# Hybrid attention and MoE step on one Trainium2 core: the sample's rows first in the last projection block

## The reference, cut to what matters

```
z = hn @ w_in
fq, fk, fv, ff, dq, dk, dv = jnp.split(z, SPLITS, axis=-1)
...
dk = _rope(_rms(dk.reshape(n_b, n_t, DIFF_HEADS, 2, HEAD_DIM), dk_g), pos)
dk = dk.reshape(n_b, n_t, DIFF_HEADS, 2 * HEAD_DIM)
dv = dv.reshape(n_b, n_t, DIFF_HEADS, 2 * HEAD_DIM)
```

## Time and profile before

| What | us |
|---|---|
| median of three runs | 1353.77 (1352.5 to 1355.65) |
| the profiled execution, its own time | 1354.91 |
| its span, first to last instruction | 1353.0 |
| TensorE busy | 1288.7 |
| VectorE busy | 377.3 |
| ScalarE busy | 209.9 |
| GpSimd busy | 145.0 |

### The profile page before, as it was taken

How to read it: one execution, slowest core, us unless ns; L and a number is a source line. 1 busy time by engine, 2 the same in 40 slices (tenths; PEclk the granted TensorE clock), 3 DMA queues, 4 the chain that set the end, 5 groups by cost and what they waited for, 6 DMA issues and landing times.

```text
span 1353.0 us, 16150 instructions
## 1 busy us (share of the span) xinstructions
PE 1288.7 (95%) x6083; PEld 573.3 (42%) x6084; DVE 377.3 (28%) x958; ACT 209.9 (16%) x524; POOL 145.0 (11%) x340
## 2 busy tenths in 40 slices
PE   6799999999998999999999999999999999999997
PEld 3344444565454433434344343443434344343432
DVE  3213223557252322213222121311212132121212
ACT  5111322346150101101001010100101010010100
POOL 0021300000004101011010110101011010101000
PEclk9899965579998999999999999999999999999998
DMA  8901440036525999999999999999999999999994
GB/s 286 323 29 74 174 168 1 0 128 226 209 70 210 431 427 427 428 429 429 428 430 428 428 429 429 428 428 430 428 428 430 428 429 428 430 428 427 429 426 183
DMA packets 54537, 447.06 MB, mean 330 GB/s; under 512 B 10817, under 2 KB 11090, under 8 KB 29922
## 3 DMA queue, kind: packets, MB, share of 16 engines
q1 hardware_dynamic: 54498, 446.54, 79.4%
HBM read 441.66 MB, written 4.86 MB: 330 GB/s over the span
## 4 chain that ended last, share of the span: by engine, by line
PE 65%; DMA 25%; SPq 4%; DVE 2%; POOL 1%; issue 1%; ACT 1%; DVEq 0%; POOLq 0%; ACTq 0%
DMA arena<-in_w_gate_up 23%; PE psum L1588 17%; PE psum L1556 16%; PE psum L1537 7%; PE psum L1303 5%; PE psum L1451 3%; PE psum L1407 3%; PE psum L1603 2%; PE psum L1359 2%; SPq L390 2%; PE psum L1387 1%; PE psum L1339 1%; PE psum L1571 1%; PE psum L1567 1%; PE psum L1355 1%; SPq L406 1%
## 5 line engine op out<-in xcount | busy, mean ns | idle before, releaser
L1556 PE MATMUL psum<-arena 128*64 128x512 f32 x2048 | 450.5, 599 | 18.9 <-DMA arena<-in_w_gate_up 18.4
L1556 PEld LDWEIGHTS psum<-arena 128*64 128x64 f32 x2048 | 152.9, 138 | 314.7 <-issue 314.7
L1588 PE MATMUL psum<-arena 128*64 128x512 f32 x1024 | 224.8, 597 | 0.8
L1210 DVE TENSOR_SCALAR arena<-psum 128x256 f32<-128x256 f32 x64 | 26.7, 418 | 432.4 <-PE psum L1556 430.6
L1588 PEld LDWEIGHTS psum<-arena 128*64 128x64 f32 x1024 | 78.8, 138 | 136.0 <-issue 134.6
L1303 PE MATMUL psum<-arena 128*128 128x512 f32 x288 | 127.6, 599 | 0.0
L838 ACT ACTIVATE arena<-arena 128x256 f32<-128x256 f32 x64 | 26.7, 418 | 630.5 <-DVE arena L1210 630.5
L1537 PEld LDWEIGHTS psum<-arena 128*128 128x128 f32 x768 | 88.5, 194 | 16.1 <-issue 16.1
L1537 PE MATMUL psum<-arena 128*128 128x128 f32 x768 | 91.6, 279 | 3.8 <-POOL arena L604 3.8
L1603 PE MATMUL psum<-arena 128*128 128x512 f32 x192 | 93.2, 623 | 0.0
L597 POOL COPY arena<-arena 128x6 f32 (+1 forms) x16 | 3.0, 188 | 775.6 <-PE psum L1588 703.5
(11 more groups left out here) (215 smaller groups left out, 905.2 us busy)
## 6 DMA issues: line engine op xcount, KB each, us to landing
arena<-in_w_gate_up SPq DMA_DIRECT2D x128, 2048.0 KB, 25.0
arena<-in_w_down SPq DMA_DIRECT2D x64, 2048.0 KB, 22.6
arena<-in_w_in SPq DMA_DIRECT2D x6, 2048.0 KB, 19.6
arena<-in_cache_fox_k SPq DMA_DIRECT2D x8, 512.0 KB, 3.5
arena<-in_cache_diff_k SPq DMA_DIRECT2D x8, 512.0 KB, 4.4
arena<-in_cache_fox_v SPq DMA_DIRECT2D x8, 512.0 KB, 4.0
arena<-in_cache_diff_v SPq DMA_DIRECT2D x8, 512.0 KB, 5.6
arena<-in_w_out SPq DMA_DIRECT2D x4, 1024.0 KB, 7.5
```

Source lines behind the costliest of these rows:

```text
L1556: last = mm(banks[n][half], XT[u][:, k, half], piece_slot(s[x])[:, c0:c0 + 512], start=False, stop=(k == 7), skip_group_check=True)
L1588: last = mm(banks[hf][half], actT[:, 4 * i + c, half], w, start=False, stop=(i == 1 and c == 3), skip_group_check=True)
```

## The change

The last projection block takes its tiles in the order 3, 1, 2 in place of 1, 2, 3: unit 19 is now the sample's rows, 20 and 21 the prompt's. The transposes of unit 17, the meta rows' differential keys, come behind unit 20 in place of unit 21.

```diff
         units += [(bi, *BLOCKS[bi][1:], 0) for bi in META_BLOCKS]
-        units += [(5, *BLOCKS[5][1:], t) for t in (1, 2, 3)]
+        units += [(5, *BLOCKS[5][1:], t) for t in (3, 1, 2)]
         NU = len(units)
...
-                newest = u - 1 if u < meta0 else -1 if u < meta0 + 4 else meta0 if u < NU - 1 else u
+                newest = u - 1 if u < meta0 else -1 if u < meta0 + 4 else meta0 if u < NU - 2 else u
```

## The result

The changed kernel takes 1361.45 us, the median of 20 runs (1354.25 to 1363.8). Beside them the kernel before took 1355.34 us (20 runs, 1352.5 to 1357.71). The ratio is 1.0038 with a 95% interval of 1.0026 to 1.005, which is 3.5 to 6.8 us slower, 5.1 by the ratio and 6.1 by the medians. The profiled execution took 1360.66 us, its span is 1358.7 us, 5.7 more than before.

What follows compares the result with a forecast made beforehand. The prediction took a fixed-length weight stream from the first refill as the bound, so earlier delays count in full. Waits of 4.70 us plus 1.9 for the clock made 6.6 us, giving 1360.4 us, range 1356.8 to 1364.5.

Steps and rivals of the forecast that it cites:

- What bounds the kernel: From the first refill at 427.12 us a weight stream of fixed length sets the end; earlier delays count in full.
- The wait for the rotation: After unit 20, PE waits for unit 17's rotation on GpSimd until 171.83 us; 3.3 us of PE are lost.
- The copy behind the store: ScalarE's copy of the sample's rows waits for unit 17's store, ending at 174.05 us; unit 21 slips 5.56 us.
- What leaves the end of the projection: Unit 17's transposes and ScalarE's copy, formerly behind unit 21, now lie under the wait, taking off 0.74 us.
- The clock: PE's pause before unit 21 lowers the clock; the unit's first 3.85 us run at half speed, costing 1.9 us.
- The first rival: The wait is there, but the clock holds or is given back in attention: 1356.8 to 1358.5 us, chance 0.20.
- The sum: Whole kernel: 4.70 + 1.9 = 6.6 us slower, 1360.4 us against the median of 1353.77, chance 0.62.
- 4.70 for the waits alone: Start of attention: first scores 4.82 us later, less 0.12 us no longer held by the first exponential, makes 4.70 us.
- Store caught behind the weights: Unit 17's store is overtaken by the 2 MB weight load; the slip grows by 6.7 us: 1367 us, chance 0.06.
- Absorbed: The DMA stream starts by something other than PE's first pieces, so the delay vanishes: 1353.8 us, chance 0.08.
- Faster by the clock in attention: Shifted start leaves the clock high in prompt attention, deciding at 9.4 us more: 1349.1 us, chance 0.04.
- Stores and later loads at nothing: The sample's earlier store, the prompt's later one and the later weight load behind unit 21 cost nothing.

Runs made afterwards that it cites:

- e5_dose: Kernel before plus 8 calls (16 passes) of matmuls nobody reads, behind unit 17's transposes and ahead of attention: ratio 1.0047, 6.4 us slower.
- e11_route2: Kernel before plus matmuls nobody reads in two idle places of PE behind the output projection, one call and two calls: ratio 0.9983, 2.3 us faster.
- e2: Kernel before with tile order 3, 1, 2, the sample's values in their own buffer, and unit 17's transposes behind unit 20: ratio 1.0016, 2.2 us slower.
- e3: Kernel before with only unit 17's transposes moved one unit sooner, behind unit 20: ratio 1.0021, 2.8 us slower.
- e10_late: Kernel before with order 3, 1, 2, own buffer for sample's values, unit 17's transposes behind first scores, unit 18's store ahead of the 2 MB load: 0.9983.
- e1_spare: Kernel before with order 3, 1, 2, the sample's values in their own buffer, and unit 17's transposes left behind unit 21: ratio 0.9999.
- e6_fill1: Kernel before plus one call (2 passes of 512 columns) of matmuls nobody reads in each step of prompt attention: ratio 1.0232, 31 us slower.
- e4_warm: Changed kernel plus matmuls nobody reads in the pause, 4 calls behind unit 20 and one behind the transposes: ratio 1.0048 against the kernel before.
- e9_warm_again: Same kernel as e4_warm, timed again beside the changed kernel on one chip: ratio 1.0039 against the kernel before.

## Why the prediction was right, point by point

- **What bounds the kernel.** Right in the main. By the timed runs e5_dose carried a known delay to the end, and e11_route2 took a gain from the same stretch to the end. The stream behind the first refill is not of fixed length, though: 924.6 to 928.5 us over the 14 traces. That the first refill moved by 6.68 us, with 6.6 forecast, is in part luck. The execution was 0.31 us late before unit 19 began, the delay was down to 5.4 us at the last FoX scores, and 1.0 us came on top behind them, where the clock rose at about 293 us in place of 288.
- **The wait for the rotation.** Forecast 3.3 us, 3.17 measured, with GpSimd's L564 as the releaser. e2 and e3 show its share of the total, the low clock that follows it included: 2.2 and 2.8 us.
- **The copy behind the store.** Forecast: store lands in 1.6 us and the copy ends 2.2 us behind the rotation. Measured 1.6, and 174.47 - 172.14 = 2.33. The slip of unit 21 against unit 19 is 5.67 us, 5.56 forecast. The figure of about 2.0 us of the Trainium skill, DMA: Bandwidth & Descriptors, section on the anatomy of one DMA, would have given an estimated 6.0. The page gives that figure for transfers issued from GpSimd, and here SP issues. This store took 1.6 us in every trace where it was read, so the measurement decides.
- **What leaves the end of the projection.** The forecast 0.74 us are confirmed by e10_late, where the same work left that place: first scores 0.73 us sooner.
- **The clock.** The direction is right and the size off. The term was 1.9 us in unit 21, and 2.75 and 2.87 were measured; the low level lasted from 173.3 to 180.1, 5.6 us of it in the unit, where the row that I took it from had 3.85. I gave nothing back, and the trace shows it given back: the high level held for 6.0 us of attention in place of 2.5. From the first to the third scores the kernel needed 3.80 us, before 5.19, which is 1.4 us back, and at the last FoX scores the delay is 5.4 us, where it was 7.7 at the first scores. The first rival had this as a case of its own, with "clock holds, or is given back" as alternatives to the fall; both happened in one execution.
- **The sum.** 6.6 us forecast, 5.1 (3.5 to 6.8) by the ratio, 6.1 by the medians. 4.70 for the waits alone would have fitted as well, and the runs can't tell the two apart. The fit owes something to two errors that pull opposite ways: the low clock cost 0.9 us more in unit 21 than forecast, and 2.3 us came back in attention, for which the sum had nothing.
- **The rivals.** Store caught behind the weights: no, 1.6 us in every trace of the change. Absorbed: no. Faster by the clock in attention: no, the high level lasted 3.5 us longer than before. The 9.4 us of the prediction are mis-worked: a microsecond at the high level does the work of two at the low one and so gives back up to a whole one, and the rival was to decide at 4.7 us, not 9.4. The 3.5 us gave back 2.3 of the 7.7. Stores and later loads at nothing: e1_spare, 0.9999.

## What to carry to other kernels

Before reordering work so that a store goes sooner, look at which buffer it now writes and who lay in it: a buffer shared by turns makes the new first comer wait for the last user's transposes and for the landing of its store. A delay ahead of the first transfer of a saturated stream reached the end in full here, within intervals of some 2 us, and so did a gain. Where TensorE pauses anyway and the clock falls, matmuls that nobody reads can hold it if they fit into the pause; where it is already full at the low level they only add.

## What the runs showed of the hardware that was not expected

- Prompt attention keeps PE nearly full for 100 us at the lower clock of 1.2 GHz. With two passes of 128 x 512 more in each step (2.1 of some 5.7 us in e6_fill1) the FoX half still stayed low for 85 us.
- A table load of 1.28 us was followed by the exponential 0.01 to 0.02 us later, in the changed kernel and in e10_late.
- A 32 KB store issued ahead of a 2 MB load landed in 1.6 us, one issued 0.47 us behind the load in 8.2 to 8.3 us, before and after. In e10_late both stores went ahead of the load: the first landed in 1.6 us, the second, issued 0.46 us ahead of the load, in 3.3.
- One trace is not the total. e4_warm and e9_warm_again are the same kernel and agree within 0.1 us up to the last FoX scores; then the clock rose at about 283 us in the one and 291 in the other. Over all traces that rise lay between 278 and 295 us. So one profiled execution can lie some microseconds off its kernel's median, as that of e5_dose does (1356.22 against 1360.86).
